# Mixer stage: when the convolution's SiLU, softplus, the states' exponentials and a norm's end are issued

## The reference, cut to what matters

```python
def centred_dwconv_silu(u, w, b):      # width 3, depthwise
    out = lax.conv_general_dilated(u, w[:, None, :], (1,), 'SAME', ...)
    return jax.nn.silu(out + b)

def softplus_dt(dt_raw, dt_bias):      # 24 columns: 2 directions x 12 heads
    return jax.nn.softplus(dt_raw.reshape(b, L, 2, SSD_HEADS) + dt_bias)
```

## Time and profile before

| | |
|---|---|
| median of 3 runs | 3566.09 us (3564.87 to 3566.77) |
| profiled execution, its own time | 3565.38 us |
| its span | 3564.1 us |
| mean granted PE clock | 0.991 |

### The profile page before, as it was taken

The page is one execution under the profiler, slowest core; times in us unless marked ns, Lnnn a source line. Parts: engine busy times, 40 slices in busy tenths (PEclk is TensorE's granted clock), DMA queues, the critical chain, the costliest instruction groups (busy, mean ns, idle before and its releaser), DMA issues.

```text
span 3564.1 us, 44801 instructions
## 1 busy us (share of the span) xinstructions
PE 3456.8 (97%) x17264; PEld 2749.1 (77%) x17264; DVE 1653.8 (46%) x3091; ACT 1431.5 (40%) x2426; POOL 1225.3 (34%) x549
## 2 busy tenths in 40 slices
PE   6999999888999999999999999999999999999999
PEld 4888899776688887877776788887877776778887
DVE  7977466557420115655542333232855453234132
ACT  3223455554532223354443344343354453344242
POOL 2554200000044443434332444444434333334443
PEclk9999999999999999999999999999999999999999
DMA  8565365221123323222222222323322222223332
GB/s 316 192 225 192 125 189 165 71 84 54 48 89 89 101 89 103 84 71 89 83 77 82 84 89 92 99 92 110 100 76 84 78 74 89 83 83 97 98 94 85
DMA packets 118564, 376.42 MB, mean 106 GB/s; under 512 B 15440, under 2 KB 16336, under 8 KB 117968
## 3 DMA queue, kind: packets, MB, share of 16 engines
q1 hardware_dynamic: 115872, 367.88, 32.5%
q10 hardware_dynamic: 2480, 5.68, 0.5%
HBM read 359.86 MB, written 2.10 MB: 102 GB/s over the span
## 4 chain that ended last, share of the span: by engine, by line
PE 87%; DVE 6%; ACT 4%; issue 1%; DMA 1%; POOL 0%; SPq 0%; ACTq 0%; DVEq 0%; POOLq 0%
PE ps L1423 26%; PE ps L1425 25%; PE ps L1424 25%; PE ps L1683 2%; PE ps L1702 2%; ACT b L1765 1%; PE ps L1665 1%; PE ps L1466 1%; DVE b L2192 1%; PE ps L1661 1%; PE ps L1725 1%; PE ps L1736 1%; PE ps L1474 1%; DVE b L2355 1%; DVE b L2260 0%
## 5 line engine op out<-in xcount | busy, mean ns | idle before, releaser
L2682 POOL TENSOR_TENSOR b<-b,b 128x1024 fp32r<-128x1024 f32 (+1 forms) x501 | 1156.0, 2307 | 2268.9 <-ACT b L1765 2266.0
L1423 PE MATMUL ps<-b,b 128*128 128x512 f32 (+1 forms) x4720 | 1792.2, 380 | 48.2 <-DVE b L2192 15.4
L1425 PE MATMUL ps<-b,b 128*128 128x512 f32 (+1 forms) x4720 | 1754.0, 372 | 0.0
L1424 PE MATMUL ps<-b,b 128*128 128x512 f32 (+1 forms) x4720 | 1753.3, 371 | 0.0
L1423 PEld LDWEIGHTS ps<-b,b 128*128 128x128 f32 x4720 | 889.9, 189 | 278.0 <-issue 81.0
L1425 PEld LDWEIGHTS ps<-b,b 128*128 128x128 f32 x4720 | 890.2, 189 | 160.4
L1424 PEld LDWEIGHTS ps<-b,b 128*128 128x128 f32 x4720 | 891.0, 189 | 155.9 <-issue 5.8
L1765 ACT ACTIVATE b<-b 128x1024 fp32r<-128x1024 f32 (+2 forms) x622 | 607.1, 978 | 323.8 <-PE ps L1425 313.6
L2317 DVE CUSTOM_DVE_ANT_0 b<-b,b,b 128x1024 bf16<-128x1024 f32 x112 | 223.5, 1996 | 32.3 <-DMA b<-in_ada 21.4
L1826 ACT ACTIVATE b<-b 128x512 fp32r<-128x512 f32 (+1 forms) x110 | 64.8, 589 | 371.1 <-DVE b L2236 268.5
L2192 DVE TENSOR_TENSOR b<-b,b 128x1024 fp32r<-128x1024 f32 (+2 forms) x121 | 135.4, 1122 | 109.7 <-ACT b L1765 109.4
(11 more groups left out here) (236 smaller groups left out, 2406.6 us busy)
## 6 DMA issues: line engine op xcount, KB each, us to landing
b<-in_w SPq DMA_DIRECT2D x458, 512.0 KB, 3.5
b<-in_ada SPq DMA_DIRECT2D x88, 512.0 KB, 5.3
b<-in_w SPq DMA_DIRECT2D x80, 384.0 KB, 3.1
b<-in_w SPq DMA_DIRECT2D x80, 320.0 KB, 2.9
b<-b SPq DMA_DIRECT2D x176, 64.0 KB, 2.0
b<-in_const SPq DMA_DIRECT2D x24, 256.0 KB, 3.9
b<-in_x SPq DMA_DIRECT2D x2, 1024.0 KB, 12.0
out<-b SPq DMA_DIRECT2D x8, 256.0 KB, 2.0
```

What stands on the lines that cost most here:

```text
L1423: pe.matmul(out, a[0], b[0], start=first, stop=False)
L1424: pe.matmul(out, a[0], b[1], start=False, stop=False)
L1425: return pe.matmul(out, a[1], b[0], start=False, stop=last)
L2682: then(pool.tensor_tensor(wlo[j % NS][:, 0:nk * w], raw[j % NR][:, 0:nk * w], whi[j % NS][:, 0:nk * w].bitcast(F32), ALU.subtract), "lop", j)
```

## The change

Four things move; no arithmetic is added or taken away. (1) The SiLU (`cv3`) becomes a step of its own, which `begin` puts out right behind itself (list `F.next`): ACT's order is centre tap, `split` of the next `begin`, SiLU. The last of `xb` goes behind the `begin` of `cdt`, the last of `cx` behind that of `uf`. (2) `sp` becomes three background steps: part 0 up to DVE L2163, with ACT's Exp and Ln; part 1 from the reciprocal on; part 2 what follows the softplus. (3) The four `ccol` become one background item, and they and `cwg` stand ahead of the `grp` steps. (4) In the background of `xb` three of the gaps stand between `squares(5)` and `prenorm(3)`, so that the `nfin` of norm 5 comes later; four gaps stand ahead of `col`, and the rate is 0.52.

```diff
@@ Fore.begin
         self.step("begin", c=c)
+        while self.next:
+            self.items.append((self.next.pop(0), 0.0))
+def soft_steps(key):
+    return [do("sp", s=key, part=part) for part in range(3)]
@@ schedule, xb
         F.step("evac", t=t)
+        F.next.append(do("cv3", t=t))
-    S += weave(F, addnorm(1) + squares(5) + prenorm(3) + [do("sp", s="x")] + [do("gap")] * 6 + [do("col")], 0.5)
+    last, F.next = F.next, []
+    S += weave(F, addnorm(1) + squares(5) + [do("gap")] * 3 + prenorm(3) + soft_steps("x") + [do("gap")] * 4 + [do("col")], 0.52)
     F = fore()
+    F.next = last
     F.narrow("cdt", "cdt", ("pn", 3), LC, 24)
@@ schedule, cx
         F.step("evac", t=t)
+        F.next.append(do("cv3", t=t))
+    end, F.next = F.next, []
-    S += weave(F, [do("row"), do("gap"), do("sp", s="c")] + [do("grp", g=g) for g in range(4)]
-               + [do("ccol", i=i, d=d) for i in range(2) for d in range(2)] + [do("cwg")], 0.5)
+    S += weave(F, [do("row"), do("gap")] + soft_steps("c") + [[do("ccol", i=i, d=d) for i in range(2) for d in range(2)]]
+               + [do("cwg")] + [do("grp", g=g) for g in range(4)], 0.5)
     F = fore()
+    F.next = end
     F.tm("uf", 1, "uf", ("pn", 2), 4)
@@ act_program (was the end of evac)
+            elif k == "cv3":
+                at.wait_ge(*n("cv2", name, i))
+                act.activation(out, o[:, 0:N], ACT.Silu).then_inc(up("cv3", name, i), 1)
-            elif k == "sp" or k == "fg1":
+            elif (k == "sp" and st["part"] == 0) or k == "fg1":
@@ dve_program
-        def softplus(key):
+        def softplus_in(key):
 ...
             own(dve.tensor_scalar(d, w, -1.0, 1e-30, ALU.add, ALU.max))
+        def softplus_out(key):
             at.wait_ge(*n("spa", key, 1))
             own(dve.reciprocal(w, d))
 ...
-                if st["s"] == "x":
-                    at.wait_ge(*n("dt"))
-                    softplus("x")
+                if st["part"] == 0:
+                    at.wait_ge(*n("dt" if st["s"] == "x" else "cdt"))
+                    softplus_in(st["s"])
+                elif st["part"] == 1:
+                    softplus_out(st["s"])
+                elif st["s"] == "x":
                     at.wait_ge(*n("nal"))
```

More of the change, by code:

```diff
@@ L215, in __init__ @@
     def __init__(self, stream, at):
-        self.stream, self.at, self.items, self.tail, self.late = stream, at, [], [], []
+        self.stream, self.at, self.items, self.tail, self.late, self.next = stream, at, [], [], [], []
     def step(self, kind, cost=0.0, **kw):
@@ L743, in number @@
                 mark(*t["freed"])
-                mark("cv3", name, i)
             elif name == "z":
@@ L832, in number @@
             mark("tc", s["s"], s["m"])
+        elif k == "cv3":
+            mark("cv3", s["t"]["name"], s["t"]["i"])
         elif k == "sp":
-            soft(mark, s["s"])
-            if s["s"] == "x":
+            if s["part"] == 0:
+                soft(mark, s["s"])
+            elif s["part"] == 1:
+                mark("spx", s["s"])
+            elif s["s"] == "x":
                 mark("da")
@@ L948, in number @@
             soft(mark, ("f", s["l"]))
+            mark("spx", ("f", s["l"]))
             mark("lfs", s["l"])
@@ L1036, in soft @@
     mark("spa", key, 1)
-    mark("spx", key)
 class Waits:
@@ L1842, in act_program @@
                                    scale=pv("conv_w", 14 + ch)).then_inc(up("cv1", name, i), 1)
[L1843 to L1849, removed]
                 elif name == "z":
@@ L1961, in act_program @@
                         up("tc", "c", m), 1)
-            elif k == "sp" or k == "fg1":
+            elif k == "cv3":
+                name, i, N = st["t"]["name"], st["t"]["i"], st["t"]["N"]
+                o = Q[(i if name == "xb" else 14 + i) % 4]
+                at.wait_ge(*n("cv2", name, i))
+                out = o[:, 0:N]
+                if name == "xb" and i < 4:
+                    out = cT[:, i, :]
+                elif name == "xb" and i >= 10:
+                    out = bT[:, i - 10, :]
+                act.activation(out, o[:, 0:N], ACT.Silu).then_inc(up("cv3", name, i), 1)
+            elif (k == "sp" and st["part"] == 0) or k == "fg1":
                 key = st["s"] if k == "sp" else ("f", st["l"])
@@ L2163, in softplus @@
             own(dve.tensor_scalar(d, w, -1.0, 1e-30, ALU.add, ALU.max))
+        def softplus_out(key):
+            x, (ab, u, w, d) = soft_of(key)
             at.wait_ge(*n("spa", key, 1))
@@ L2392, in dve_program @@
                 else:
-                    at.wait_ge(*n("cdt"))
-                    softplus("c")
                     for i in range(2):
@@ L2527, in dve_program @@
                 at.wait_ge(*n("lf", l))
-                softplus(("f", l))
+                softplus_in(("f", l))
+                softplus_out(("f", l))
                 own(dve.memset(flat_mg[:, 2048:2560], 0.0))
```

## The result

| | before | changed |
|---|---|---|
| median (range, executions) | 3565.48 us (3560.38 to 3566.77, 4) | 3544.97 us (3537.83 to 3546.47, 4) |
| profiled execution / span | 3565.38 / 3564.1 | 3546.27 / 3544.9 |
| mean granted PE clock | 0.991 | 0.992 |

The ratio is 0.9941 with a 95% interval of 0.9924 to 0.9958: the change makes the kernel 20.5 us faster. The forecast was 3544.

The account below looks back on a forecast made before the run. PE, busy 97% of the span, bounds the kernel; only its stops and lower clock can be won. Gains 5.5+7.2+1.2+7.8 = 21.7 us from 3565.38 leave 3543.7, adjusted to the median 3544; range 3535 to 3555.

Parts of the forecast that it names:

- The mechanism and the ceiling: Mixer: centre tap, side taps, SiLU, high and low half are a relay idling ACT and DVE; 31.6 us could be won.
- Norm 5 and softplus of x: In `xb`: gains of 5.5 us at norm 5, a 1.2 us stop remaining, and 7.2 us at softplus of x.
- `col` and `cdt`: `col` moves behind chunk 13; its 34 thin matmuls left at their cost, between nothing and 2 us either way.
- `cx`: Gain 1.2 us: old stops cost 7.8, new ones 6.6 (2.0 at `ccol`, 2.9 for chunk 5's bank, 1.7 clock).
- The table loads: Near the end of `cx`: four `ccol` loads and their SiLU loads become one each, 5.1 us of ACT.
- Entry of `uf`: PE stands 2.1 us at `h0`, without a clock loss, instead of 7.58 plus 2.3 clock: gain 7.8 us.
- X: Stretch from the first `xb` matmul to the first `cx` matmul; 12.7 us forecast for it.
- C: Stretch: first `cx` matmul to first `h0`, 6.7 us forecast. Rival: SiLU behind `split`'s DMA wait, slower, 3573; chance 0.03.
- U: Stretch from the first `h0` to the first matmul of `z`; 2.3 us forecast for it.
- A: Rival: ACT and DVE run so far ahead that the new stops close too, 31.6 us: 3534.5; chance 0.13.
- B: Rival: DVE's own work sets the pace, so norm 5 keeps its stop; 12.7 us, 3553; chance 0.19.
- D: Rival: side taps, not SiLU, held the relay; only table loads and `cwg` help `uf`, 5 to 8 us: 3559; chance 0.05.

Follow-up runs that it names:

- silu_only: Changed kernel with SiLU's new place kept and the other three parts taken back: 3540.94 us, ratio 0.9932 to before.
- silu_back: Changed kernel with SiLU back in its old place, the other three parts kept: 3568.34 us, ratio 1.0007 to before.
- best: Changed kernel with one bank and one Exp for `ccol`, gaps ahead of `ccol` and `h0`, and `xb`'s background as before the change: 3531.09 us, ratio 0.9910.
- all_fixed: Changed kernel with one bank and Exp for `ccol`, one gap more ahead of it, three ahead of `h0`, one gap moved into `squares(5)`: 3532.46 us, ratio 0.9908.
- sp_whole: Changed kernel with the three softplus parts run as one step, for x and for c: 3545.82 us, one execution.
- norm_early: Changed kernel with the three gaps moved from ahead of `prenorm(3)` to behind softplus: 3543.07 us, one execution.
- after_again: Changed kernel run once more, unedited: 3544.14 us, ratio 0.9945 to before.
- ccol_back: Changed kernel with `grp` ahead again and four single `ccol` steps behind it: 3544.63 us, one execution.
- one_bank: Changed kernel with the four `ccol` results in one PSUM bank, read by a single Exp: 3538.23 us, one execution.
- ccol_single: Changed kernel with the four `ccol` as single background steps, still ahead of `grp`: 3539.70 us, one execution.

## Why the prediction was right, point by point

- **The mechanism and the ceiling.** ACT and DVE were late through their order, not their load: shown by `silu_only` and `silu_back`. Of the 31.6 us that could be won, 20.5 were; `best` wins 33.3 against its own runs of before (3564.34), more than the 31.6, since part of it lies outside the stage. In the stage alone `all_fixed` wins 31.1 and `best` 29.3.
- **Norm 5 and softplus of x.** 12.7 us were forecast for the two; PE reached `cdt` 11.9 us sooner (99.38 to 87.44 us from the first `xb` matmul). The residual stop was 1.19 where 1.2 was forecast, and it cost no clock, as assumed. But this gain belongs to SiLU's place. The text said that the softplus needed the slack and priced it at 3.5 us without; with the slack, neither its division nor the later norm's end shows any worth (`sp_whole`, `norm_early`), and rate 0.52 opens the 1.19 us stop that `silu_only` does not have.
- **`col` and `cdt`.** `col` was left "at their cost, between nothing and 2 us either way". From `cdt` to `cx` it was 1.1 us more than before in the profiled execution, 0.9 less in `after_again` and 1.5 more in `ccol_back`, by the clock alone. The prediction's sum of clock losses also leaves out that `cdt` ran partly at the lower clock in the kernel before, with no stop just ahead of it.
- **`cx`.** Both new stops are at their places with the waiting instructions named, smaller than forecast: 1.12 for 2.0, 2.23 for 2.9. The first ended 17.5 us after the first `cx` matmul, where the softplus was put (17.6), and the bank of chunk 3, for which the forecast added time up to 18.6, held nothing up: the twelve short matmuls of `ccol` run 1.3 us without a gap. At the second PE arrived at 20.0 (19.9 forecast) and went on at 22.2 (22.8). The clock behind them cost 2.3 for 1.7, and it was charged to the wrong stop: it had fallen before the second one, and fell in `one_bank` without it. From the first `cx` matmul to `h0`, 6.7 us were forecast (1.2 and the shorter stop at `uf`), 8.1 measured.
- **The table loads.** 8 and 3 became 6 and 1 as forecast, each 1.283 us. The first Exp starts 1.29 us after its load (720.09 to 721.38), so the row, and not the 2.66 us that the Trainium skill gives for a switch (ScalarE: Activation LUTs, What ACT_TABLE_LOAD costs), held again. But the sum gained nothing from them that the banks did not take.
- **Entry of `uf`.** A stop of 2.59 for 2.1. This is where a term failed: "again without a clock loss". The clock fell to 0.69 and lost 1.7 us, so U shrank by 0.55 us and not by 2.3. Its ground, that only the long stops are followed by the lower clock, doesn't hold (last section).
- **The sum** was 21.7 and the stage gave 19.5. X gave 10.9 where 12.7 was forecast for it, C 8.1 for 6.7 and U 0.6 for 2.3: errors of both signs that partly cancel. The other execution of the changed kernel gave 23.2, with its X 3.2 us shorter by the clock. That 3544.97 lies within 1 us of 3544 is therefore luck in part; the terms were good to 1 or 2 us each.
- **The rivals.** A (every stop goes, 3534.5) did not happen by itself, but `best` and `all_fixed` come out within 4 us of it, though up to 4 us of that are not the stops. B: DVE did not set the pace, it waits for centre taps, 32.7 us in 20 waits. C: one `split` waits for its DMA, 1.2 us, where two did before. D is refuted by `silu_only`.

What the bundle hides is that three of the four parts do not pay. In the stage they cost 3.0 us (`silu_only` against `after_again`, both at the full clock from `col` to `cx`; 1.2 of them are the stop at norm 5 and 2.0 lie in C) to 6.7 (against the profiled changed kernel); the whole times agree in sign (3540.94 against 3544.14 and 3544.97), but their intervals overlap, so by time alone this isn't shown.

## What to carry to other kernels

Where two engines hand work back and forth and neither is full, look in the groups view at what ended each one's idle time; if an engine that works strictly in order waits for its partner while the partner's next input stands behind that wait, put the input first: here it was worth the whole gain, with no instruction changed. When small steps are grouped, count the banks that they take between two uses of the same one, and when items of a rate-driven list are joined or split, keep the places of those behind them with gaps. Take a bundled change apart once it works; here its best part alone did at least as well, and moving a few steps to close the stops that were left took 6 to 12 us off the changed kernel's stage. And before a small gain in one trace is put down to an edit, look how much the parts that nobody edited differ between traces; here it was up to 6 us.

## What the runs showed of the hardware that was not expected

Between `col` and `cx` PE is never idle in any of these kernels, and still its clock differs between executions of one order of work. From the first `xb` matmul to `col` eight traces take the same 82.5 us, within 0.03. Then comes the stretch from `cdt` to `cx`: 24 matmuls with 24 columns of weights and 256 positions each; the counts take in one to three neighbours. In the changed kernel, `ccol_back`, `one_bank` and `silu_only`, one row each:

```profile
696.57:701.37 4.80, 4.80 (x27) 0.56 0.12 24
```

```profile
698.01:703.23 5.22, 5.22 (x27) 0.50 0.13 42
```

```profile
696.62:699.45 2.83, 2.83 (x26) 1.00 0.01 3
```

```profile
694.45:697.21 2.76, 2.76 (x25) 1.00 0.00 0
```

The same work takes 2.8 us at 2.4 GHz and up to 5.2 at 1.2 GHz. The changed kernel shows both in two executions: 4.80 here, 2.83 in `after_again`, and with `col` (4.94 and 3.71) this is the whole 3.2 us by which their X differ. `silu_only` and `best`, which have one order up to there, show it too (X 87.75 and 90.92). What decides it in an execution stays open; no experiment was made on it.

The second surprise is how unevenly short stops are paid. The 1.19 us at norm 5 cost no clock in any kernel that has it. The 1.1 us at `ccol`, with the twelve short matmuls of all four `ccol` behind it, was followed by the lower clock in all five traces that have it so (0.66 in `one_bank`). In `ccol_single` the stop is the same, 1.11 us, but only four such matmuls stand right behind it, and the clock stayed at 1.00:

```profile
716.13:721.10 4.97, 4.97 (x42) 1.00 0.53 160
```

Nor did it fall there behind three more stops, of 1.2, 1.1 and 0.7 us. So the length of a stop does not tell what it costs; what PE does around it counts, and which property of that work it is stays open.
